# A decoder layer on one core: the relative-bias table spread by transfers of repeated rows, and the step sizes computed in four column bands

## What is computed

```
dt = softplus(dt_raw + dt_bias)          # dt_raw: x @ w_in[:, 32 columns], one step size per token and SSD head
a  = -exp(a_log) * dt
dist = query index - key index
logits[h] = q k / 8 + rel_bias[t5_bucket(max(dist, 0)), h]     where dist >= 0, else -inf
```

## Time and profile before

| | us |
|---|---|
| median of 3 runs | 1033.52 (1033.33 to 1034.95) |
| the profiled execution: its own time | 1034.76 |
| its span in the trace | 1032.5 |
| PE busy | 1004.9 |
| DVE busy | 536.6 |
| ACT busy | 376.0 |
| POOL busy | 57.3 |

### The profile page before, as it was taken

The page is one execution under the profiler, slowest core; times in us unless marked ns, Lnnn a source line. Parts: engine busy times, 40 slices in busy tenths (PEclk is TensorE's granted clock), DMA queues, the critical chain, the costliest instruction groups (busy, mean ns, idle before and its releaser), DMA issues.

```text
span 1032.5 us, 15444 instructions
## 1 busy us (share of the span) xinstructions
PE 1004.9 (97%) x6376; PEld 719.8 (70%) x6377; DVE 536.6 (52%) x1054; ACT 376.0 (36%) x660; POOL 57.3 (6%) x53
## 2 busy tenths in 40 slices
PE   8999999999999999999999999999999999999994
PEld 7999999999999899998975444444444444444432
DVE  6999455767679976665586322222222222222223
ACT  5765435555585643445231111211121112111112
POOL 0001102333200000000020000000000000000000
PEclk9999999999999999999999999999999999999998
DMA  7564534333343455648837999999999999999972
GB/s 302 195 237 148 198 123 136 134 135 128 123 174 113 163 182 187 238 170 308 349 139 304 384 417 421 421 420 419 420 419 420 420 420 421 421 420 419 420 320 82
DMA packets 41654, 290.86 MB, mean 282 GB/s; under 512 B 4712, under 2 KB 5872, under 8 KB 6896
## 3 DMA queue, kind: packets, MB, share of 16 engines
q1 hardware_dynamic: 40800, 284.62, 69.8%
q0 software_dynamic: 784, 5.24, 1.3%
HBM read 288.78 MB, written 1.06 MB: 281 GB/s over the span
## 4 chain that ended last, share of the span: by engine, by line
PE 82%; DVE 13%; issue 2%; ACT 2%; DMA 1%; SPq 0%; ACTq 0%; DVEq 0%
PE stream L1842 21%; PE stream L1523 21%; PE stream L1866 11%; PE stream L1548 8%; PE work L1831 6%; DVE w_lo L958 4%; DVE acc L994 3%; PE stream L1791 2%; DVE rms L1120 2%; PE stream L1792 1%; PE stream L1794 1%; PE stream L1796 1%; DMA raw<-in_wdense 1%; PE work L1649 1%; PE work L1625 1%
## 5 line engine op out<-in xcount | busy, mean ns | idle before, releaser
L958 DVE TENSOR_TENSOR w_lo<-raw,w_hi 128x1024 fp32r<-128x1024 f32 x142 | 171.1, 1224 | 54.4 <-ACT w_hi L666 54.3
L1842 PE MATMUL stream<-ring,xg 128*64 128x512 f32 x640 | 197.0, 592 | 0.8 <-issue 0.8
L666 ACT ACTIVATE w_hi<-raw 128x1024 fp32r<-128x1024 f32 x142 | 147.0, 1051 | 54.3 <-DMA raw<-in_wdense 39.8
L1523 PE MATMUL stream<-xT_hi,w_hi 128*128 128x256 f32 x560 | 160.3, 286 | 0.0
L1523 PE MATMUL stream<-xT_lo,w_hi 128*128 128x256 f32 x560 | 157.9, 282 | 0.0
L1523 PE MATMUL stream<-xT_hi,w_lo 128*128 128x256 f32 x560 | 157.8, 282 | 0.0
L1842 PEld LDWEIGHTS stream<-ring,xg 128*64 128x64 f32 x640 | 63.0, 137 | 91.5 <-issue 90.4
L1523 PEld LDWEIGHTS stream<-xT_hi,w_hi 128*128 128x128 f32 x560 | 106.1, 189 | 4.1 <-issue 2.9
L1523 PEld LDWEIGHTS stream<-xT_hi,w_lo 128*128 128x128 f32 x560 | 105.9, 189 | 0.0
L1523 PEld LDWEIGHTS stream<-xT_lo,w_hi 128*128 128x128 f32 x560 | 105.7, 189 | 0.3 <-issue 0.2
L1400 DVE TENSOR_TENSOR hh<-h,stream 128x256 f32<-128x256 f32 x32 | 13.5, 420 | 172.3 <-ACT h L887 172.3
(11 more groups left out here) (376 smaller groups left out, 2075.5 us busy)
## 6 DMA issues: line engine op xcount, KB each, us to landing
ring<-in_wstream SPq DMA_DIRECT2D x120, 1024.0 KB, 14.8
raw<-in_wdense SPq DMA_DIRECT2D x73, 1024.0 KB, 4.8
place_e<-in_wstream SPq DMA_DIRECT2D x24, 1024.0 KB, 15.9
place_m<-in_wstream SPq DMA_DIRECT2D x12, 1024.0 KB, 13.6
place_c<-in_wstream SPq DMA_DIRECT2D x12, 1024.0 KB, 15.2
place_w<-in_wstream SPq DMA_DIRECT2D x12, 1024.0 KB, 14.7
place_x<-in_wstream SPq DMA_DIRECT2D x12, 1024.0 KB, 16.3
ln<-in_lnp POOLq DMA_DIRECT2D x3, 1024.0 KB, 7.0
```

Source lines behind the costliest of these rows:

```text
L666: nc.scalar.activation(w_hi[:, q % ROUNDED, :], raw[:, q % 6, :], ACT.Copy).then_inc(w_rounded, 1)
L958: tt(w_lo[:, q % 6, :], raw[:, q % 6, :], w_hi[:, q % ROUNDED, :].bitcast(F32), ALU.subtract).then_inc(w_rest, 1)
L1523: last = mm(S[n % 4][:, 0:SEQ], w[:, b, :], a[:, kb, :], start=(kb + j == 0), stop=(kb == chunks * KB - 1 and j == len(parts) - 1))
L1842: last = mm(S[2][e * SLOTS:(e + 1) * SLOTS, :], feature_block(buf, kb)[:, col + e * SLOTS:col + (e + 1) * SLOTS], tiles[e][kb // 4][:, kb ...
```

## The change

**The bias table.** `rel_scratch` now has 128 copies of each head's row: SP writes `bds` with every row repeated 128 times (8 x 128 x 384 numbers, 1.57 MB, where it was 12 KB), at the same place, before tile 8. SP then reads `rel` directly: partition p takes, in copy p, the window that starts at 127 - p (a step of 383 from one partition to the next). This read stands behind tile 12 instead of behind tile 8. The four `flip` products, ACT's four copies, `rel_flipped` and the two waits on them are gone; DVE waits for the read itself before the attention.

**The step sizes.** The weights are no longer split. PE makes 8 products in plain fp32 of 32 columns of weights each, into four bands of 32 partitions of bank W[1]: band g sums contraction blocks 2g and 2g+1. DVE copies all 128 partitions, and the two transposes are replaced by two plain fp32 products with `four_ident`, a 128 x 32 matrix of four stacked identities, which turns and adds the bands at once. DVE makes `four_ident` once with a reduction, behind L983. ACT's rounding of the weights (L703) and DVE's L980 are gone, and PE waits for `small_in` where it waited for L980.

```diff
-        rel_scratch = nc.dram_tensor("rel_scratch", [DIFF_HEADS, 384], F32, kind="Internal").ap()
+        rel_scratch = nc.dram_tensor("rel_scratch", [DIFF_HEADS, P, 384], F32, kind="Internal").ap()
...
                 if m == 7:
                     sp.wait_ge(rel_cp, 1)
-                    sp.dma_start(rel_scratch, bds[0:DIFF_HEADS, :]).then_inc(rel_ld, 16)
-                if m == 8:
+                    sp.dma_start(rel_scratch, bds[0:DIFF_HEADS, :].unsqueeze(1).to_broadcast([DIFF_HEADS, P, 384])
+                                 ).then_inc(rel_ld, 16)
+                if m == 12:
                     sp.wait_ge(rel_ld, 16)
-                    sp.dma_start(rel_flipped[:],
-                                 bass.AP(rel_scratch.tensor, 0, [[1, P], [384, DIFF_HEADS], [1, SEQ]])
+                    sp.dma_start(rel[:],
+                                 bass.AP(rel_scratch.tensor, P - 1, [[383, P], [384 * P, DIFF_HEADS], [1, SEQ]])
                                  ).then_inc(rel_ld, 16)
...
                     act.wait_ge(small_in, 48)
-                    nc.scalar.activation(wdt_r[0][:], w_dt, ACT.Copy).then_inc(x_rounded, 1)
...
                 leave("k", h, kT[:, h, :])
-            for k in range(4):
-                act.wait_ge(flip_mm, k + 1)
-                nc.scalar.activation(rel[:, 2 * k:2 * k + 2, :], W[k][:].rearrange("p (h k) -> p h k", h=2), ACT.Copy
-                                     ).then_inc(flip_cp, 1)
...
-                ve.wait_ge(x_rounded, 3)
-                tt(wdt_r[1][:], w_dt, wdt_r[0][:].bitcast(F32), ALU.subtract).then_inc(x_rest, 1)
                 ve.wait_ge(small_exp, 2)
                 link(stt(neg_lam[:], lam_e[:, 1:2], -LAM_INIT, lam_e[:, 0:1], ALU.add, ALU.subtract))
                 link(ts(exp_alog[:], exp_alog[:], -1.0, None, ALU.mult))
+                link(nc.vector.tensor_reduce(four_ident[:], ident.rearrange("p (g h) -> p h g", g=4), AX.X, ALU.add))
...
-            nc.vector.tensor_copy(dtT[0:SSD_HEADS, :], W[1][0:SSD_HEADS, 0:SEQ]).then_inc(dtT_cp, 1)
+            nc.vector.tensor_copy(dtT[:], W[1][:, 0:SEQ]).then_inc(dtT_cp, 1)
...
-            ve.wait_ge(flip_cp, 4)
+            ve.wait_ge(rel_ld, 32)
...
-            pe.wait_ge(x_rest, 3)
-            for kb in range(KB):
-                for j, (w, a) in enumerate(((0, 0), (0, 1), (1, 0))):
-                    last = mm(W[1][0:SSD_HEADS, 0:SEQ], wdt_r[w][:, kb, :], xT_r[a][:, kb, :], start=(kb + j == 0),
-                              stop=(kb == KB - 1 and j == 2))
+            pe.wait_ge(small_in, 48)
+            for half in range(2):
+                for band in range(4):
+                    kb = 2 * band + half
+                    last = mm(W[1][band * SSD_HEADS:(band + 1) * SSD_HEADS, 0:SEQ], w_dt[:, kb, :], xT[:, kb, :],
+                              start=(half == 0), stop=(half == 1))
...
-                        last = nc.tensor.transpose(W[1][:, SEQ + t * SSD_HEADS:SEQ + (t + 1) * SSD_HEADS],
-                                                   dtT[0:SSD_HEADS, t * P:(t + 1) * P], ident[0:SSD_HEADS, 0:SSD_HEADS])
+                        last = mm(W[1][:, SEQ + t * SSD_HEADS:SEQ + (t + 1) * SSD_HEADS],
+                                  dtT[:, t * P:(t + 1) * P], four_ident[:], start=True, stop=True)
...
-            pe.wait_ge(rel_ld, 32)
+            feature_major("k", 6, xT_r)
+
             pe.wait_ge(rel_cp, 1)
             pe.wait_ge(a_done, 1)
-            for k in range(4):
-                mm(W[k][:], flip, rel_flipped[:, 2 * k:2 * k + 2, :], start=True, stop=True).then_inc(flip_mm, 1)
-            feature_major("k", 6, xT_r)
-
-            pe.wait_ge(flip_cp, 4)
             mm(W[0][:, 0:SSD_HEADS], strict, a_v[:, 0, :], start=True, stop=True).then_inc(end_mm, 1)
```

More of the change, by code:

```diff
@@ L199, in layer_kernel @@
         slot_of = tiny("slot_of", [P, TB, EXPERTS])
+        four_ident = sb("four_ident", [P, SSD_HEADS], at)
         gates_e = tiny("gates_e", [P, TB, EXPERTS])
@@ L223, in layer_kernel @@
         xT_r = (sb("xT_hi", [P, KB, SEQ], XH, F32R), sb("xT_lo", [P, KB, SEQ], A, F32R))
-        wdt_r = (sb("wdt_hi", [P, KB, SSD_HEADS], L, F32R), sb("wdt_lo", [P, KB, SSD_HEADS], L + KIB, F32R))
         dtT = sb("dtT", [P, SEQ], L + 2 * KIB)
@@ L228, in layer_kernel @@
         rel = sb("rel", [P, DIFF_HEADS, SEQ], G)
-        rel_flipped = sb("rel_flipped", [P, DIFF_HEADS, SEQ], H)
         ln1 = sb("ln1", [P, 2, D], Z + 8 * KIB)
@@ L327, in layer_kernel @@
         strict = cs[:, C_STRICT:C_STRICT + P]
-        flip = cs[:, C_FLIP:C_FLIP + P]
         ones = cs[:, C_ONES:C_ONES + P]
@@ L361, in layer_kernel @@
         rel_mm = sem("rel_mm")
-        flip_mm = sem("flip_mm")
         dt_mm = sem("dt_mm")
@@ L397, in layer_kernel @@
         small_exp = sem("small_exp")
-        flip_cp = sem("flip_cp")
         seg_exp = sem("seg_exp")
```

## The result

The changed kernel takes 1058.06 us (median of 4 runs, 1056.74 to 1059.4), the kernel before 1034.09 us beside it (4 runs, 1033.33 to 1034.95): a ratio of 1.0232, 95% interval 1.022 to 1.0245. It is 24 us slower. The forecast was 1054.6 us, in a range of 1031.5 to 1066.

The account below looks back on a forecast made before the run. DVE bounds the kernel to 89 us, then PE to the attention stage. Flips -3.43, step sizes 0, clock +1.7, turning +0.30, write +22.5 sum to +21.1 us on 1033.5: 1054.6 us, range 1031.5 to 1066.

Parts of the forecast that it names:

- The write of 1.57 MB, +22.5 us: In SP's queue ahead of tile 8: the write delays DVE's split of chunk 16, +22.5 us (0.3 to 48.5), chance 0.68.
- W: Time of the 1.57 MB write, taken as 30 us between 3.5 and 56; DVE's chain moves back by W - 7.5 us.
- tile 8 waits until the write has left: SP's queue goes in order, so tile 8 (chunks 16 and 17), directly behind the write, waits until the write has left.
- the two signs that were to show the forecast wrong: Chunk 16's rounding starts before 56 us, or small packets of the write flow beside those of tile 8.
- Both rivals with a short write: Write between tiles 7 and 8 is short: 1032.7 us at reduced clock, chance 0.23; 1030.7 us at full clock, chance 0.09.
- the rival: Short write ahead of tile 8, reduced clock: DVE moves 0.3 to 1.3 us, sum -1.1 to -0.1 us, chance 0.23.
- The flip products, -3.43 us: In PE's gapless stretch before block k6: removing four products saves 3.43 us, as what stands behind them is ready early.
- The step sizes, 0: Eight fp32 products before q0 take 0.86 to 3.44 us; PE waits for DVE's copy anyway: 0, at most +0.1 us.
- DVE behind block 8: Removing L980 on DVE gives 0 to 0.35 us, taken as 0, since the next step also waits for ACT's exponentials.
- The reduction, +0.3 us on DVE: New reduction on DVE behind L983: +0.3 us on DVE's chain, not counted because a longer wait follows.
- The turning, +0.30 us: Behind DVE's copy of the step sizes: two fp32 products take 0.60 us where two transposes took 0.30, +0.30 us.
- The clock, +1.7 us: PE's gap before the turning grows to about 2.6 us; then 3.4 us at half clock cost +1.7 us.

Follow-up runs that it names:

- the two kernels with the bias half alone: Kernel before with only the bias-table half, write from 128 partitions: 1032.81 us; the same with ACT's decay exponential ahead of the next tile's rounding: 1031.35 us.
- four of the kernels above: The change with the write on ACT's queue (1044.86 us), from spaced partitions (1035.37), with sixteen copies and eight reads (1036.72), or from 128 partitions with two ACT exponentials moved (1032.77).
- three others: The change with the write from 128 partitions (1035.24 us) or in eight pieces (1035.56 us); the kernel before with the step-size half alone (1038.16 us).

## Why the prediction was right, by its steps

- **The write of 1.57 MB, +22.5 us: right, and its size nearly, by luck.** W was taken as 30 us and is 32.4. No row gave the 30: it was the middle of bounds of 3.5 and 56 us, and that W lies within 2.4 us of it is luck. That a write in front of tile 8 would stall the kernel for as long as it lasts was reasoned; how long it would last was not. The formula put the split of chunk 16 at 47.7 + W = 80.1; it is at 80.69. The stall is 25.5 us. That tile 8 cannot land before the write has left, that nothing catches up to the turning, and that the write's rate is near 52 GB/s (48.5) all came out. Only half of the step "tile 8 waits until the write has left" holds by its own words: half of it passes, which helps no one, as ACT needs the whole. So one of the two signs that were to show the forecast wrong did come, small packets of the write beside those of tile 8, and the forecast was right all the same: the sign was badly chosen. It had taken the queue as one line, where the other half of the engines goes on. Both rivals with a short write are out for this kernel. They are what happens with the rows spaced: there the write takes 8.7 us and the time is 1.5 us over before, where the rival had 1.1 to 0.1 us below it; the two small terms below that I missed make most of the difference.
- **The flip products, -3.43 us: wrong for this kernel, by 1.1 us.** The products are worth that, the removal here is not. PE's span from the pass to k7 shrank by 2.3 us only. The step that said that what stands behind them is ready early looked at chunk 38 and DVE. It missed ACT's exponential behind the rounding of the next tile, which the flips had covered. So 1.1 us are given back here, and 1.32 us at k7 (1.46 us of the medians) between the two kernels with the bias half alone.
- **The step sizes, 0: right where it was put.** The 16 records of the eight products took 1.07 us, against the 0.86 estimated for bands side by side and 3.44 for one after the other. PE waited for DVE's copy all the same.
- **DVE behind block 8: wrong in sign.** I gave the removed subtraction (L980) a gain of 0 to 0.35 us and did not ask what the removed *rounding on ACT* had stood in front of. It cost 1.5 us by way of the table load. In the change the stall of 25 us swallowed it (DVE waits for chunk 16 in any case), so the total did not suffer. Where the write is short it counts in full: with the spaced partitions DVE's copy begins 1.9 us later than before, and the rival had 0.3 to 1.3. With the 1.1 us of the exponential that is 1.7 to 2.7 us, about what that rival was too low by.
- **The reduction, +0.3 us on DVE, 0 in the sum:** 0.40, and hidden by the longer wait behind it, as said. **The turning, +0.30 us:** +0.33, four records as said.
- **The clock, +1.7 us: wrong here.** The gap in front of the turning was put at 2.6 us, and over 2 us was named as a sign of being right. It is 1.26 us, and the clock stays at full speed behind it; 288 products took 34.27 us:

```profile
114.89 0.63 PE L1568 MATMUL work<-four_ident,dtT 128*128 128x32 f32 x4 [1.26 <-DVE dtT L995]
```

  A reading that fits and is not tested: behind the restart at 82 us PE had a clock of 0.50 until some 86 us and ran later against DVE than before. The fall is there in four of the kernels above, at 1.4 to 1.5 us, and missing in three others, so the term was right in size and wrong in its condition, the length of the gap.
- **The read of `rel`, 0:** no trace of it on the chain in the change.

The sum of +21.1 us was 2.9 us short of the 24.0 between the medians, and 3.2 us short of the 24.3 between the two spans, which can be split: the write's stall +3.1, the flips' return +1.1, the clock -1.7, and 0.7 us between k7 and the end, of which the sum had nothing. The cause is the predicted one. The smaller terms were wrong both ways and nearly cancel, which is luck too.

## What to carry to other kernels

A transfer's price is set by where its source rows lie, by how long it is in one piece and by who is behind it: 1.57 MB from partitions 0 to 7 cost 24 us ahead of a tile that was needed, and next to nothing from 128 partitions, from 8 spaced ones, or cut into pieces that fit the time for which the queue is empty between tiles. Before an instruction is removed, look at what it stood in front of on its own engine and what it gave time to on the others: a table load fell behind a wait (1.5 us), and an exponential behind the rounding of a late tile (1.3 us), and each ate over a third of the 3.4 us to be had. And a change that saves an engine work may open a gap in front of its next product; whether the clock falls there is worth as much as either, and the length of the gap did not tell it here.

## What the runs showed of the hardware that I had not expected

- Eight reads of 16 partitions took more of the queue than one of 128 for the same bytes: 8.6 us at 125 ns a packet against 3.7 us at 46 ns. ACT waited 4.58 us for the tile behind them. In the kernel with the write from 128 partitions its longest wait in that stretch was 0.97 us.
- The write of eight partitions held about half of the engines: half of each of three tiles passed it, the rest did not, and alone it took 45.5% of the engines' time.
- Behind a tile, pieces of 196 KB from partitions 0 to 7 went mostly at 65 ns a packet, where the same piece with nothing right ahead of it had 232 ns.
- Slow packets hold up a transfer on another queue as well: with the write on ACT's queue 4 us passed (51 to 55) in which 49 GB/s flowed, all of it the write.
- The same idle time (2.10 and 2.11 us) is followed by a clock of 0.50 in one kernel's execution and by full clock in another's; 1.52 us was followed by the fall and 1.86 us was not.
